# Expert gates of a PEER layer: indirect accumulating transfers in place of one-hot products

## What is computed

```python
v1, i1 = lax.top_k(s1, PEER_TOPK)
v2, i2 = lax.top_k(s2, PEER_TOPK)
cand = (v1[..., :, None] + v2[..., None, :]).reshape(...)
cand_idx = (i1[..., :, None] * PEER_N_KEYS + i2[..., None, :]).reshape(...)
top_s, top_pos = lax.top_k(cand, PEER_TOPK)
expert = jnp.take_along_axis(cand_idx, top_pos, axis=-1)
gate = jax.nn.softmax(top_s, axis=-1)
u = jnp.take(peer_u, expert, axis=0)
act = jax.nn.gelu(jnp.einsum('chkd,cd->chk', u, zc))
v = jnp.take(peer_v, expert, axis=0)
w = (gate * act.astype(jnp.float32)).astype(zc.dtype)
return jnp.einsum('chk,chkd->cd', w, v).astype(zc.dtype)
```

## Time and profile before

| | |
|---|---|
| runs before, us | 3178.8 median of 3 (3178.67 to 3183.27) |
| the profiled execution | 3183.27 us; its span is 3183.2 us |
| PE busy | 3152.5 us, 99%, 18258 instructions |
| DVE, ACT, POOL busy | 2158.3, 1707.0, 573.2 us |
| chain of waits | PE 89%, DVE 6% |
| weights read | 572.59 MB on SP's queue, 57.0% of the 16 DMA engines |

### The profile page before, as it was taken

One profiled execution on the slowest core, in us unless ns is written; L12 is line 12 of the kernel. 1 busy time (PEld: TensorE's weight loads), 2 busy tenths in 40 slices (PEclk: granted clock), 3 DMA queues, 4 the chain that ended last, 5 costly groups with the idle time before them and its releaser, 6 DMA issues.

```text
span 3183.2 us, 47051 instructions
## 1 busy us (share of the span) xinstructions
PE 3152.5 (99%) x18258; PEld 2756.9 (87%) x18258; DVE 2158.3 (68%) x3073; ACT 1707.0 (54%) x2637; POOL 573.2 (18%) x623
## 2 busy tenths in 40 slices
PE   8999999999999999999999999999999999999999
PEld 7888889888888888888888888888888888888887
DVE  8957999855646565555646579999775856555554
ACT  6654567544545454454545655665656544444454
POOL 0023200221313132221313410000241000000003
PEclk9999999999999999999999999999999999999999
DMA  6565567766666666666656655555655656666564
GB/s 245 166 205 177 181 192 246 240 216 191 206 198 191 212 190 214 188 216 187 216 187 191 188 189 170 178 176 173 189 189 167 194 189 191 188 190 191 188 190 139
DMA packets 177998, 615.36 MB, mean 193 GB/s; under 512 B 18288, under 2 KB 35056, under 8 KB 176496
## 3 DMA queue, kind: packets, MB, share of 16 engines
q1 hardware_dynamic: 157824, 572.59, 57.0%
q10 hardware_dynamic: 19952, 39.76, 3.6%
HBM read 593.41 MB, written 18.87 MB: 192 GB/s over the span
## 4 chain that ended last, share of the span: by engine, by line
PE 89%; DVE 6%; issue 2%; ACT 1%; POOL 1%; DMA 0%; POOLq 0%; ACTq 0%; DVEq 0%
PE G L458 57%; PE G L462 29%; DVE lo L1142 2%; PE M L570 2%; DVE CV L1487 1%; DVE tS L1152 1%; DVE tS L1148 0%; POOL X L1697 0%; POOL acc L1702 0%; ACT hi L744 0%; PE M L537 0%; PE M L551 0%; ACT tQ L773 0%; DVE oneB L1456 0%; DVE eq L1427 0%
## 5 line engine op out<-in xcount | busy, mean ns | idle before, releaser
L458 PE MATMUL G<-ZA,hi 128*128 128x512 f32 x5104 | 1779.0, 397 | 15.8 <-DVE lo L1142 10.2
L1142 DVE TENSOR_TENSOR lo<-raw,hi 128x1024 fp32r<-128x1024 f32 x1088 | 1378.9, 1289 | 285.7 <-ACT hi L744 285.0
L462 PE MATMUL G<-ZA,lo 128*128 128x256 f32 x5120 | 1390.0, 278 | 0.0
L458 PE MATMUL G<-ZB,hi 128*128 128x512 f32 x3568 | 1241.7, 395 | 0.0
L744 ACT ACTIVATE hi<-raw 128x1024 fp32r<-128x1024 f32 x1088 | 1117.4, 1052 | 80.5 <-DMA raw<-in_pv 42.3
L458 PEld LDWEIGHTS G<-ZA,hi 128*128 128x128 f32 x5104 | 945.5, 188 | 221.0 <-issue 12.8
L462 PE MATMUL G<-ZB,lo 128*128 128x256 f32 x3584 | 989.8, 278 | 0.0
L462 PEld LDWEIGHTS G<-ZA,lo 128*128 128x128 f32 x5120 | 966.1, 189 | 19.7
L458 PEld LDWEIGHTS G<-ZB,hi 128*128 128x128 f32 x3568 | 665.9, 188 | 154.4 <-DVE ZB L1261 0.3
L751 ACT ACTIVATE tA<-G 128x256 f32<-128x256 f32 x558 | 212.7, 382 | 949.2 <-PE G L462 948.4
L462 PEld LDWEIGHTS G<-ZB,lo 128*128 128x128 f32 x3584 | 674.6, 188 | 4.4
(11 more groups left out here) (304 smaller groups left out, 1325.3 us busy)
## 6 DMA issues: line engine op xcount, KB each, us to landing
raw<-in_pu SPq DMA_DIRECT2D x256, 512.0 KB, 4.2
raw<-in_pv SPq DMA_DIRECT2D x256, 512.0 KB, 4.2
raw<-in_w_in SPq DMA_DIRECT2D x192, 512.0 KB, 3.6
raw<-in_w_up SPq DMA_DIRECT2D x128, 512.0 KB, 3.6
raw<-in_w_down SPq DMA_DIRECT2D x128, 512.0 KB, 3.7
raw<-in_w_out SPq DMA_DIRECT2D x32, 512.0 KB, 3.5
raw<-in_wq SPq DMA_DIRECT2D x32, 512.0 KB, 3.6
g_scratch<-stage ACTq DMA_DIRECT2D x16, 1024.0 KB, 4.8
```

The lines of the kernel that those rows point to most:

```text
L458: pe.matmul(G[:, 0:512], w, Z[:, k, :], start=first, stop=False, skip_group_check=True)
L462: m = pe.matmul(G[:, 0:256], lo[POS[u][p] % NRAW][:, k % 8, :], weights(u, p)[1][:, k, 0:256], start=False, stop=last, skip_group_check=True)
L1142: dve.tensor_tensor(lo[r][:, :, :], raw[r][:, :].rearrange("p (k n) -> p k n", k=8), hi[w][:, :, :].bitcast(F32), ALU.subtract).then_inc(s ...
```

## The change

The gate matrix in DRAM becomes a flat list of single numbers, [expert, token]. ACT clears it by 16 transfers of 1 MB in units 43 to 58. DVE turns the chosen key indices into flat addresses (`token_column`, `place`). POOL then issues 256 indirect transfers, each of which adds 128 gates, one per token, to the addresses in one column of IDX. The two token halves t take turns, 16 transfers at a time; within a half, the next head waits until the transfers before have landed. One-hots, their products, transposes and staging go.

To give these transfers time, the first products of five groups (KEPT) stand in a row, units 56 to 135, and their second products after, units 136 to 215; three groups alternate in units 216 to 311. Groups 2 to 4 are written to h_scratch, unit by unit, and come back by `load_h`. POOL multiplies all five by the gate (`gate_kept`); before, DVE did it for group 0 (`gate_a`) and POOL for group 1. PHASED, SCALE_V and ROUTE_AT follow.

```diff
-UB = [56, 72] + [120 + 32 * c for c in range(6)]
-VB = [88, 104] + [136 + 32 * c for c in range(6)]
+KEPT = 5
+UB = [56 + 16 * c for c in range(KEPT)] + [56 + 32 * c for c in range(KEPT, 8)]
+VB = [56 + 16 * KEPT + 16 * c for c in range(KEPT)] + [b + 16 for b in UB[KEPT:]]
-SCALE_V = list(range(OT)) + list(range(UB[0], UB[0] + 11)) + list(range(F0, MG))
+SCALE_V = list(range(OT)) + list(range(UB[0], VB[0])) + list(range(F0, MG))
-PHASED = [19, OT + 1, VB[0] + 2, VB[1] + 1, VB[1] + 3] + UB[2:] + VB[2:] + [VB[7] + 2, MG, YO + 1, M0 + 3, M0 + 17, M0 + 19] + [
+PHASED = [19, OT + 1, VB[0] + 2] + UB[KEPT:] + [v + 1 for v in VB[1:]] + [MG, YO + 1, M0 + 3, M0 + 17, M0 + 19] + [
-ROUTE_AT = {61: ((0, 0),), 62: ((1, 0), (2, 0)), 63: ((0, 1), (1, 1)), 64: ((2, 1), (0, 2)), 65: ((1, 2), (2, 2)),
-            66: ((0, 3),), 68: ((1, 3),), 69: ((2, 3),)}
+ROUTE_AT = {61: ((0, 0),), 62: ((1, 0), (2, 0), (3, 0)), 63: ((0, 1), (1, 1)), 64: ((2, 1), (3, 1), (0, 2)),
+            65: ((1, 2), (2, 2), (3, 2)), 66: ((0, 3),), 67: ((1, 3), (2, 3), (3, 3))}
+ROUNDS = [(t, h) for h in range(8) for t in range(2)]
-        scr = nc.dram_tensor("g_scratch", [8, 128, T * 16], F32, kind="Internal").ap()
+        scr = nc.dram_tensor("g_scratch", [128 * 128 * T, 1], F32, kind="Internal").ap()
+        hscr = nc.dram_tensor("h_scratch", [KEPT - 2, 128, 16 * T], F32, kind="Internal").ap()
...
# PE: gone are spread and turn, with their calls
-                    if 68 <= u < 84:
-                        spread(2 * (u - 68))
...
# ACT
+                if st == "u" and 2 <= c < KEPT and part == 3:
+                    act.wait_ge(s_ag, 16 * c + i + 1)
+                    act.dma_start(hscr[c - 2][:, T * i:T * i + T], b[:, :]).then_inc(spilled(u)[0], 16)
+            def clear_g(n):
+                act.wait_ge(s_pad, 5)
+                size = 128 * 8 * T
+                act.dma_start(scr[size * n:size * n + size, :].rearrange("(p f) o -> p (f o)", p=128), zero[:, :]).then_inc(s_gz, 16)
+            def load_g(c):
+                size = 16 * 128 * T
+                src = scr[size * c:size * c + size, :].rearrange("(j i t) o -> i j (t o)", j=16, i=128)
+                act.dma_start(Gc[:, :, :], src).then_inc(s_gc, 16)
+            def load_h(c):
+                act.wait_ge(s_za, 8 * (c - 2) + 8)
                 for n in range(4):
+                    act.wait_ge(s_hs[n], 64 * (c - 1))
+                act.dma_start(HB[c % 2][:, :, :].rearrange("p j t -> p (j t)"), hscr[c - 2]).then_inc(s_hr[c % 2], 16)
...
+                if u == VB[0] - 8:
+                    act.wait_ge(s_sc[0], 2048)
+                    act.wait_ge(s_sc[1], 2048)
+                    load_g(0)
+                for c in range(7):
+                    if c < KEPT and u == VB[c]:
+                        act.wait_ge(s_gta, 4 * c + 4)
+                        load_g(c + 1)
+                    if c >= KEPT and u == VB[c] + 1:
+                        act.wait_ge(s_gm2, 16 * (c - KEPT + 1))
+                        load_g(c + 1)
+                for c in range(2, KEPT):
+                    if u == VB[c - 2] + 1:
+                        load_h(c)
...
# DVE
+            def place(n):
+                t, half = divmod(n, 2)
+                dve.wait_ge(s_sel, n + 1)
+                if half == 0:
+                    dve.wait_ge(s_ixa, 3)
+                    dve.tensor_scalar(IXF[:, t, :], tpf[:, 0, :], float(T), tcol[:, t:t + 1], ALU.mult, ALU.add).then_inc(s_ixa, 1)
+                else:
+                    dve.wait_ge(s_ixa, t + 4)
+                    dve.scalar_tensor_tensor(out=IDX[:, t, :], in0=tpf[:, 1, :], scalar=float(128 * T), in1=IXF[:, t, :],
+                                             op0=ALU.mult, op1=ALU.add).then_inc(s_idx, 1)
-                if 67 <= u < 83:
-                    one_hot(2 * (u - 67))
-                    one_hot(2 * (u - 67) + 1)
...
# POOL
+            def gate_kept(c, n):
+                k = slice(4 * n, 4 * n + 4)
+                B = HB[c % 2]
+                if c < 2:
+                    pool.wait_ge(s_ag, 16 * c + 4 * n + 4)
+                else:
+                    pool.wait_ge(s_hr[c % 2], 16 * (c // 2))
+                pool.wait_ge(s_gc, 16 * c + 16)
+                pool.tensor_tensor(B[:, k, :], B[:, k, :], Gc[:, k, :], ALU.mult).then_inc(s_gta, 1)
+            def scatter(t, h):
+                pool.wait_ge(s_idx, t + 1)
+                pool.wait_ge(s_sfn, 3 * t + 3)
+                if h == 0:
+                    pool.wait_ge(s_gz, 256)
+                else:
+                    pool.wait_ge(s_sc[t], 256 * h)
+                for k in range(16 * h, 16 * h + 16):
+                    pool.indirect_dma_start(scr, bass.IndirectOffsetOnAxis(IDX[:, t, k:k + 1], 0), sel[:, t, k:k + 1], None,
+                                            compute_op=ALU.add).then_inc(s_sc[t], 16)
+                if u == UB[0] + 7:
+                    for t, h in ROUNDS:
+                        scatter(t, h)
+                for c in range(KEPT):
+                    first, step = (VB[c - 1] + 4, 2) if c else (VB[0] - 6, 1)
+                    if u in range(first, first + 4 * step, step):
+                        gate_kept(c, (u - first) // step)
```

More of the change, by code:

```diff
@@ L258, in build @@
         R1, R2, R3 = (sb(f"R{i}", [128, T]) for i in range(3))
-        small = region(4096, "small_mem", [(n, [128, T], F32) for n in ("acc0", "acc1", "tQ0", "tQ1")],
-                       [("oneB0", [128, 8, 128], F32)])
-        acc, tQ = [small["acc0"], small["acc1"]], [small["tQ0"], small["tQ1"]]
+        acc, tQ = [sb(f"acc{i}", [128, T]) for i in range(2)], [sb(f"tQ{i}", [128, T]) for i in range(2)]
+        tcol = sb("tcol", [128, 2])
         tA = [sb(f"tA{i}", [128, T]) for i in range(3)]
@@ L291, in build @@
             sem(n) for n in ("s_g1", "s_con", "s_gw", "s_poolw", "s_keys", "s_mn"))
-        s_st = [sem("s_st0"), sem("s_st1")]
-        s_gh = [sem("s_gh0"), sem("s_gh1")]
+        s_gz, s_ixa, s_idx = (sem(n) for n in ("s_gz", "s_ixa", "s_idx"))
+        s_sc = [sem("s_sc0"), sem("s_sc1")]
+        s_hs = [sem(f"s_hs{i}") for i in range(4)]
+        s_hr = [sem("s_hr0"), sem("s_hr1")]
         s_gc, s_out = sem("s_gc"), sem("s_out")
@@ L553, in scores @@
                 m.then_inc(s_key, 1)
[L555 to L578, removed]
             def attention(a, step):
@@ L674, in tensor_program @@
                     scores(u - WQ - 2)
[L675 to L683, removed]
-                if u == 71:
-                    turn(0, tpf[:, 0, :], (s_sel, 3), s_spr, SPREAD_AT.index(12) + 1)
-                if u == 73:
-                    turn(1, tpf[:, 1, :], (s_sel, 4), s_spr, SPREAD_AT.index(21) + 1)
                 if u == F0 + 2:
@@ L883, in gate_split @@
             def gate_split(c, part):
[L884 removed]
                 for n in range(4 * part, 4 * part + 4):
[L886 to L895 removed]
+                    if c:
+                        act.wait_ge(s_mm, done(VB[c] - 1, part))
+                    act.wait_ge(s_gta, 4 * c + n // 2 + 1)
+                    act.activation(ZB[:, 2 * n:2 * n + 2, 0:256], HB[c % 2][:, 2 * n:2 * n + 2, :], ACT.Copy).then_inc(s_zah, 1)
             def gates(j):
@@ L1168, in ring_free @@
                     dve.wait_ge(s_ag, 16 * c + i + 1)
+                elif st == "u" and c < KEPT:
+                    dve.wait_ge(*spilled(w))
                 elif st == "gb":
@@ L1428, in gathered @@
                 if t:
-                    dve.wait_ge(s_tr, (1, 3)[half])
+                    dve.wait_ge(*((s_idx, 1) if half else (s_ixa, 4)))
                 dve.wait_ge(s_pkd, 4 * n + 4)
@@ L1578, in vector_program @@
                 for step, n in ROUTE_AT.get(u, ()):
-                    (match, pick, gathered)[step](n)
+                    (match, pick, gathered, place)[step](n)
                 if u == 62:
```

198 lines of the change are left out of this document (48 added, 150 removed).

## The result

The changed kernel takes **3245.8 us** (median of 4 runs, 3243.7 to 3247.5); the kernel before, on the same chip, takes 3178.7 (4 runs, 3178.0 to 3183.3). The ratio is 1.0209, with a 95% interval of 1.0197 to 1.0221: 2.1% slower. The forecast was 3112 us, 2.1% faster, with a range that ends at 3150. The prediction was wrong in its sign, and what came is its rival A, late scatters. The profiled execution after took 3243.7 us, with a span of 3241.7.

A forecast was written before the change was run, and what follows sets the result against it. PE, busy 99% of 3183.2 us, was taken as the bound; less 63.6, 0.6, 0.7 and 3, plus 0.5, gave 3115.8 us, or 3111.4 against the median, forecast as 3112 us, range 3100 to 3150.

The forecast's parts named there:

- rival A: POOL's scatters late, held up by DVE: costs from 1.4 us each, 3263 us at 2 us; chance 0.12 beyond 1.67 us.
- The scatters: POOL's 256 indirect transfers from 405.5 us, needed by about 766: about 1 us each, free up to 1.4 us.
- The upper end of 4.2 us: One scatter at a time from issue to landing, like a 512 KB weight; would add 715 us.
- The rule for the cost: Scatters needed by about 766 us: up to 1.4 us each costs nothing, beyond it each 0.1 us costs 25.6 us.
- PE work removed: One-hot products in units 68 to 83 go, 63.6 us; six transposes, 0.6 us; units 84 to 89 faster, 0.7 us.
- The pace: Slow product groups in units 136 to 311: gain of 3 us, between 6.5 us gained and 11.4 us lost.
- Rival B: The product stream keeps the slow pace in all of units 136 to 311: 3126 us; chance 0.08.
- Work at nothing: Added or moved DVE, ACT and POOL work, clears, spills and borders stay hidden; 0.5 us charged for units 61 to 68.
- Sum: 3183.2 - 63.6 - 0.6 - 0.7 - 3 + 0.5 = 3115.8 us; against the median 3111.4, forecast 3112 us.

The follow-up runs named there:

- seven groups: The changed kernel with KEPT = 7 instead of 5, so seven groups' first products stand up front: 3112.0 us against 3179.5 before, ratio 0.9785.

## Why the prediction was wrong

**The step that failed** is the price in "The scatters": "I take about 1 us". It measured 1.88 us, 1.54 on POOL and the rest between two. The reasons given for 1 us were about other things. That 16 go out without a wait between them and that a landing is covered were both right and gave nothing, since the time for which each instruction holds POOL is the limit. "An engine whose 128x256 operation costs 0.744 us" says what arithmetic costs, not what one transfer does: twice the elements add only 0.133 us to 1.407. The upper end of 4.2 us was a bound and the lower end, ACT's 0.37 us, too; the value between them was chosen nearer to the lower end without a row of POOL issuing anything. With bounds of 0.37 and 4.2 us and a threshold at 1.4, a chance of 0.12 for rival A was too small.

The Trainium skill (DMA: Bandwidth & Descriptors, Latency and other measured facts), which puts about 1 us before the first byte for a POOL-issued transfer, was read as if it were the price of one of many in a row. The trace has 1.54 us with the addition and 0.96 without it, each plus 0.30: near it only for the plain write.

**The rule for the cost held.** The threshold, "up to (766 - 405.5) / 256 = 1.4 us", and the slope of 25.6 us per 0.1 us give, with 1.88 us, an end 256 x 1.88 - 360.5 = 121 us late. PE was idle for 126.0: 2.9 us of the difference are the start, 408.4 and not 405.5. The 3.6 us of slower work behind the stop were not in the rule. "ACT waits for all 256 in unit 128's turn" (750, it was 752) and the PE stop "at 769" (769.87) were right.

**Rival A's mechanism was only half right.** It made the scatters late by DVE's hold on POOL. Up to 440 us, where DVE works without a gap on the routing and then on late splits, 12 of the 15 scatters take 1.6 to 2.6 us; but from 800 to 850, with DVE idle, 28 of them have 41.77 us in the window, and from 750 to 800, with DVE at 3.30 us, 41.76. Between 506 and 750, DVE 59% busy, the median is 1.540 and the longest 1.637. Over all 256 the mean is 1.567 against a median of 1.540, so what delayed single ones added 7 us of the 121. The Trainium skill (SBUF — State Buffer, Who interferes with whom) has a VectorE instruction with two SBUF inputs and a GpSimd one that reads SBUF lock each other out. For the scatters the trace can show that up to 440 us and seldom later, and with 64 elements, where single ones take 1.83 instead of 1.41 us while DVE splits weights. The price of 1.54 us stands without DVE and without weights, so neither makes it.

**PE work removed: right.** Units 68 to 83 took 88.74 us with seven groups, forecast 88.84, and 152.43 before: -63.7.

**The pace: right in sign, too small.** I took 3 us between bounds of -6.5 and +11.4. All of the 6.5 us came: with seven groups, units 168 to 183 took 88.79 us where the earlier trace rows have 90.41, and no group between 136 and 311 is slow, with five groups nor with seven. Rival B (all slow) is out.

**Work at nothing: right.** From unit 56 to 67 the seven-group kernel took 67.56 us, and I had charged 0.5 us for it; the same 12 units took 68.29 before (the window 349.16 to 417.45), so it gained 0.7. The clears, spills and borders cost nothing that the runs can tell. POOL's gate products took 2.42 us in the median, not 2.918, and a DVE split beside them went up to 3.43 as one did before (3.61).

**Sum.** Without the wait the terms give 3111.4; with seven groups, where there is no wait, it measured 3112.0. That the two lie so close is in part luck: between the profiled executions, on which the terms were worked out, the gain was 3183.2 - 3109.2 = 74.0 us and not 67.4 (of the 6.6 more, 3.5 are the pace and 1.2 units 56 to 67), and the profiled execution of before was the longest of its four. One term at 1.88 instead of 1 turned -67 into +67.

## What to carry to other kernels

Before a loop of small transfers moves to an engine that the trace has never seen issue one, get the price of one instruction: the few hundred in a row here were priced by the time that each held that engine, not by bytes, elements or landings. If no row has it, work out the break-even price first (here 1.4 us), and if that lies inside the bounds, give both sides a real chance. A cheaper instruction is not safe either: plain writes at 0.96 us ended in time and held up PE. And a wait that comes from a fixed late date is cured by moving its reader past the date (two more groups of independent work), while moving the wait to another queue gave 6 us of 126.

## What the runs showed of the hardware

- An indirect accumulating transfer of 128 elements of 4 bytes holds POOL 1.54 us, one of 64 elements 1.41 (1.54 in the mean beside the product stream), a plain write of 128 elements 0.96, each with 0.30 us before the next.
- Beside plain ones 1.26 us apart PE issued one instruction every 1.4 us, 36 products in 100 us, with no wait that the profile shows and the DMA engines 0.05 busy; beside plain ones 1.87 us apart in the mean, each with a memset behind it, PE made 579 in 100 us.
- Scatters with addition keep the DMA engines at 0.23 with no other traffic (the window 800 to 850, 0 GB/s); plain ones at nearly the same rate at 0.01. Beside weights and spills at 211 GB/s that made a share of 0.91, where plain ones beside 214 GB/s had 0.77, and PE didn't wait.
- PE's clock was at 0.50 (1.2 GHz) through the idle stretch, and the first half unit after it cost 2.9 us more.
